# Sparse attention: the token's norm factor moves from the queries into distances, maximum and the exponential's scale

## What is computed

```python
z = u @ w_in
q, kc, vc, ks, vs, kw, vw, gl = split(z)
qg = q.reshape(T, 4, 4, 128) * 128 ** -0.5          # 16 heads, 4 groups
k_cmp, v_cmp = compress(kc), compress(vc)           # 15 blocks
s = qg . k - slope[head] * dist                     # for k_cmp, ks, kw; masked where dist < 0
o = g0 * softmax(s_cmp) @ v_cmp + g1 * softmax(s_slc) @ vs + g2 * softmax(s_win) @ vw
```

## Time and profile before

| what | value |
|---|---|
| median of 3 executions | 3325.81 us |
| profiled execution, its time | 3326.84 us |
| its span | 3325.1 us |
| PE busy | 3297.8 us, 99% |
| PE weight loads busy | 2792.7 us, 84% |
| DVE busy | 1981.9 us, 60% |
| ACT busy | 1570.3 us, 47% |
| TensorE's granted clock | 1.0 in all 40 slices |

### The profile page before, as it was taken

How to read it: one execution, slowest core, us unless ns; L and a number is a source line. 1 busy time by engine, 2 the same in 40 slices (tenths; PEclk the granted TensorE clock), 3 DMA queues, 4 the chain that set the end, 5 groups by cost and what they waited for, 6 DMA issues and landing times.

```text
span 3325.1 us, 40632 instructions
## 1 busy us (share of the span) xinstructions
PE 3297.8 (99%) x16736; PEld 2792.7 (84%) x16736; DVE 1981.9 (60%) x2606; ACT 1570.3 (47%) x2168; POOL 66.3 (2%) x67
## 2 busy tenths in 40 slices
PE   9999999999999999999999999999999999999998
PEld 8888888888889888878888888888888888888887
DVE  5875665565767856674544445574778645444455
ACT  5573444454553544564444444453555534444443
POOL 0000000000001010000000000000000000000000
PEclk9999999999999999999999999999999999999999
DMA  6454445554543434455555555555423555555554
GB/s 258 157 208 184 173 151 190 182 190 171 185 177 129 156 123 152 165 195 186 190 197 195 190 179 201 190 202 187 152 103 131 194 194 190 191 192 187 197 178 157
DMA packets 84057, 592.49 MB, mean 178 GB/s; under 512 B 9313, under 2 KB 10081, under 8 KB 13345
## 3 DMA queue, kind: packets, MB, share of 16 engines
q1 hardware_dynamic: 81584, 576.23, 47.8%
q0 software_dynamic: 2288, 13.67, 1.1%
HBM read 587.76 MB, written 2.10 MB: 177 GB/s over the span
## 4 chain that ended last, share of the span: by engine, by line
PE 93%; DVE 3%; ACT 2%; issue 1%; DMA 0%; POOL 0%; SPq 0%; POOLq 0%; DVEq 0%; ACTq 0%
PE ps L2773 91%; DVE wlo L1538 1%; PE ps L3627 1%; ACT whi L673 1%; ACT sq L691 1%; PE ps L2954 0%; DVE l L2388 0%; DVE xx L1682 0%; ACT l4s L1445 0%; PE ps L3602 0%; DMA raw<-in_ev_in 0%; DVE xres L1843 0%; PE ps L3051 0%; ACT xx L770 0%; DVE l4s L2656 0%
## 5 line engine op out<-in xcount | busy, mean ns | idle before, releaser
L1538 DVE TENSOR_TENSOR wlo<-raw,whi 128x1024 fp32r<-128x1024 f32 x1089 | 1307.4, 1220 | 840.2 <-ACT whi L673 839.1
L2773 PE MATMUL ps<-whi,xx 128*128 128x512 f32 x5184 | 1655.1, 394 | 2.6 <-DVE wlo L1538 1.5
L673 ACT ACTIVATE whi<-raw 128x1024 fp32r<-128x1024 f32 x1089 | 1129.0, 1055 | 902.3 <-PE ps L2773 799.2
L2773 PEld LDWEIGHTS ps<-whi,xx 128*128 128x128 f32 x5184 | 973.6, 188 | 205.8 <-DVE wlo L1538 4.0
L2773 PE MATMUL ps<-wlo,xx 128*128 128x512 f32 x2592 | 1009.5, 389 | 0.0
L2773 PE MATMUL ps<-xx,whi 128*128 128x512 f32 (+3 forms) x2464 | 629.5, 373 | 3.1 <-ACT whi L680 2.0
L2773 PEld LDWEIGHTS ps<-wlo,xx 128*128 128x128 f32 x2592 | 487.5, 188 | 94.8
L2773 PEld LDWEIGHTS ps<-xx,whi 128*128 128x128 f32 (+2 forms) x2464 | 408.5, 187 | 51.9 <-issue 3.6
L2773 PE MATMUL ps<-xx,wlo 128*128 128x256 f32 x2160 | 378.7, 281 | 0.0
L2773 PEld LDWEIGHTS ps<-xx,wlo 128*128 128x128 f32 x2160 | 337.4, 187 | 40.4
L2773 PE MATMUL ps<-whi,fhh 128*128 128x512 f32 x704 | 274.7, 390 | 0.0
(11 more groups left out here) (367 smaller groups left out, 1690.6 us busy)
## 6 DMA issues: line engine op xcount, KB each, us to landing
raw<-in_ffn_gu SPq DMA_DIRECT2D x176, 1024.0 KB, 4.8
raw<-in_ffn_down SPq DMA_DIRECT2D x88, 1024.0 KB, 4.8
raw<-in_ab_in SPq DMA_DIRECT2D x64, 1024.0 KB, 4.8
raw<-in_ev_in SPq DMA_DIRECT2D x62, 1024.0 KB, 4.9
raw<-in_od_in SPq DMA_DIRECT2D x48, 1024.0 KB, 4.8
raw<-in_nsa_in SPq DMA_DIRECT2D x40, 1024.0 KB, 4.8
raw<-in_ev_out SPq DMA_DIRECT2D x16, 1024.0 KB, 4.8
raw<-in_od_out SPq DMA_DIRECT2D x16, 1024.0 KB, 4.7
```

The costliest lines, as they stand in the source:

```text
L673: self.e.activation(m.hi[i % NSPLIT][:, 0:w], m.raw[t % NRAW][:, off:off + w], ACT.Copy).then_inc(*self.up("hi", i))
L1538: self.e.tensor_tensor(m.lo[i % NSPLIT][:, 0:w], m.raw[t % NRAW][:, off:off + w], m.hi[i % NSPLIT][:, 0:w].bitcast(F32), SUB).then_inc(*se ...
L2773: return self.e.matmul(out, l, r, start=start, stop=stop, skip_group_check=True)
```

## The change

The queries stay as `x * gain @ w`, without the factor r of their token and without 128 ** -0.5. The scores are then too large by `1 / (r * SQ)` for each token, with SQ = 128 ** -0.5. So the slopes are divided by `r * SQ` (a column for each head and token tile, made once), the maximum is multiplied by `-r * SQ` in place of -1, and the exponential gets `r * SQ` as its scale. The multiplication L1788 falls away for the queries; the scores wait for the sum in place of the product. Masked distances are 1e27 in place of 1e32, and compressed rows that have no valid key get distance 0.

```diff
+    slopes = np.broadcast_to(-np.asarray(SLOPE2) / SQ, (128, 16))
...
-    big = 1e32
+    big = 1e27
...
-                    e.activation(ap, ap, ACT.Exp, bias=mx[:, i:i + 1], accum_out=den[:, i:i + 1]).then_inc(
-                        *self.up("l4_exp", it, i))
+                    e.activation(ap, ap, ACT.Exp, bias=mx[:, i:i + 1], scale=m.cell(2, "l4_up")[:, it % 2:it % 2 + 1],
+                                 accum_out=den[:, i:i + 1]).then_inc(*self.up("l4_exp", it, i))
...
+        if raw:
+            return
         self.wait_ge("summed", tag, nb, q, 1)
...
         self.finish()
+        self.score_factors()
         self.bg(self.attention4(), R4[0])
...
-                (self.evict_later if i else self.evict_pair)(m.l4_q[:, i * 4 + 2 * q:i * 4 + 2 * q + 2, :], "l4_q", i, q, SQ)
+                (self.evict_later if i else self.evict_pair)(m.l4_q[:, i * 4 + 2 * q:i * 4 + 2 * q + 2, :], "l4_q", i, q,
+                                                             raw=True)
...
+    def score_factors(self):
+
+        m, e = self.m, self.e
+        r, root = m.cell(2, "rs", "x4"), m.cell(2, "l4_root")
+        slope = m.cell(32, "l4_slope").rearrange("p (a h) -> p a h", a=2)
+        self.wait_ge("rstd", "x4")
+        e.reciprocal(root, r).then_inc(*self.up("l4_factor", "root"))
+        e.tensor_scalar(m.cell(2, "l4_up"), r, SQ, None, MUL).then_inc(*self.up("l4_factor", "up"))
+        e.tensor_scalar(m.cell(2, "l4_down"), r, -SQ, None, MUL).then_inc(*self.up("l4_factor", "down"))
+        self.wait_ge("l4_factor", "root")
+        e.tensor_tensor(slope, bc(m.cst[:, C_SLOPE:C_SLOPE + 16].unsqueeze(1), [128, 2, 16]),
+                        bc(root.unsqueeze(2), [128, 2, 16]), MUL).then_inc(*self.up("l4_factor", "slope"))
...
+                slope = m.cell(32, "l4_slope")[:, 16 * qt + h:16 * qt + h + 1]
                 self.wait_ge("l4_scores", it)
                 self.wait_ge("l_dm4")
+                self.wait_ge("l4_factor", "slope")
...
-                e.scalar_tensor_tensor(out=s3, in0=bc(dm[:, mo:mo + nk].unsqueeze(1), [128, 2, nk]), scalar=-SLOPE2[h],
+                e.scalar_tensor_tensor(out=s3, in0=bc(dm[:, mo:mo + nk].unsqueeze(1), [128, 2, nk]), scalar=slope,
...
-                e.scalar_tensor_tensor(out=sc, in0=dm[:, 384 + qt * 16:384 + qt * 16 + 15], scalar=-SLOPE2[h],
+                e.scalar_tensor_tensor(out=sc, in0=dm[:, 384 + qt * 16:384 + qt * 16 + 15], scalar=slope,
...
-                e.tensor_scalar(mx, mx, -1.0, None, MUL).then_inc(*self.up("l4_soft", it, "neg"))
+                e.tensor_scalar(mx, mx, m.cell(2, "l4_down")[:, qt:qt + 1], None, MUL).then_inc(
+                    *self.up("l4_soft", it, "neg"))
...
-                self.wait_ge("scaled", "l4_q", g, 1)
+                self.wait_ge("summed", "l4_q", g, 1, 1)
```

More of the change, by code:

```diff
@@ L30 @@
 C_GAIN = 128
+C_SLOPE = 144
 C_TRI = 256
@@ L65, in constants @@
     t = np.arange(128)[None, :]
-    parts = [np.eye(128), gain, np.zeros((128, 112)), s <= t, np.ones((128, 128))]
+    slopes = np.broadcast_to(-np.asarray(SLOPE2) / SQ, (128, 16))
+    parts = [np.eye(128), gain, slopes, np.zeros((128, 96)), s <= t, np.ones((128, 128))]
     for level in range(7):
@@ L85, in distances @@
             d = base + np.arange(128)[:, None] - (16 * np.arange(15)[None, :] + 31)
-            v = (d >= 0) if keep else np.where(d >= 0, d, big)
+            v = (d >= 0) if keep else np.where(d >= 0, d, np.where((d >= 0).any(axis=1, keepdims=True), big, 0))
             out += [v, np.zeros((128, 1))]
@@ L1760, in pair_block, with evict_later @@
             self.evict_pair(outs[q], tag, nb, q, scale)
-    def evict_later(self, out, tag, nb, q, scale=None):
-        self.due.append((out, tag, nb, q, scale))
+    def evict_later(self, out, tag, nb, q, scale=None, raw=False):
+        self.due.append((out, tag, nb, q, scale, raw))
     def step(self):
@@ L1773, in finish, with evict_pair @@
         self.step()
-    def evict_pair(self, out, tag, nb, q, scale=None):
+    def evict_pair(self, out, tag, nb, q, scale=None, raw=False):
         m, e = self.m, self.e
```

## The result

| | before | after |
|---|---|---|
| median of the runs (22 each), us | 3325.64 | 3330.26 |
| lowest and highest, us | 3324.43 to 3327.30 | 3328.88 to 3331.96 |
| span of the profiled execution, us | 3325.1 | 3327.1 |
| from the gates' table load to the next feed-forward's, us | 288.73 | 293.46 |

The ratio is 1.0014, with a 95% interval of 1.0008 to 1.0020: slower by 4.6 us. The interval leaves out 1, so the loss is clear, though it is smaller than the 0.2% that the prediction took as the least change that can be told. The forecast was 3331.0 us and "same".

A forecast was written before the change was run, and what follows sets the result against it. TensorE, busy 99%, is held at 15 places by a ring over three engines. VectorE's and ScalarE's added columns less the removed products, 16d+14a-1.34 = 5.2 us, on 3325.8 gave 3331.0 us, "same"; range 3326.0 to 3335.4 us.

The forecast's parts named there:

- lateness counts once a step in held places: Attention ring: at 15 places where TensorE waits, each nanosecond added counts; lateness ends where VectorE waits for TensorE's scores.
- The sum by runs: Attention stretch, walked between places where VectorE waits for TensorE's scores: added times together 5.2 us.
- a: ScalarE, each attention step: second column on three exponentials, 0.087 us each, adds 0.26 us a step.
- the second column is free: Rival, ScalarE's exponentials: second column costs nothing, about 1.5 us more in all, 3327.3 us; chance 0.13.
- the one at 0.17: Rival, ScalarE's queue: second column costs 0.17 us per exponential, 8.8 us more in all, 3334.6 us; chance 0.22.
- The third rival, that the columns are hidden: Columns cost nothing but the product's removal counts: -1.0 us, 3324.8 us; chance 0.1.
- d: VectorE, each attention step: three scalars become per-token columns, 0.06 us each, adding 0.18 us a step.
- The product: VectorE, queries: eight L1788 go, 0.72 us each; two credited in the sum, at 2350 to 2381 and at 2438.21.
- TensorE's idle time: Edited stretch: TensorE's idle time was to rise from 3.5 to about 8.7 us, most of it after 2440.
- TensorE's idle time of 3.5 us caps any gain: Edited stretch: relief of VectorE or ScalarE cannot gain more than TensorE's 3.5 us idle, so -0.2% is out of reach.
- The marks of held places: TensorE's loads 0.29 us after L2684's start (8 transposes) or 0.31 to 0.38 after L1423's (7 scores) show holds; more expected.
- Four small instructions and the slopes' wait: Ahead of the projections: four instructions of some 0.17 us hidden by VectorE's 2.09 us idle; the wait costs nothing.

The follow-up runs named there:

- e5: Kernel before with a column of ones as scale in the exponentials of attention steps 4 to 12 only: stretch -0.02 us, median 3325.56 us.
- e6: Kernel before with a column of ones as scale in the exponentials of attention steps 13 to 26 only: stretch +3.13 us, median 3328.80 us.
- e1: Kernel before with a column of ones as scale in all 96 exponentials, nothing else: stretch +3.98 us, median 3329.22 us.
- e2: Kernel before with slopes and -1 read from constant columns in VectorE's three instructions of each step, nothing else: stretch +2.11 us, median 3327.56 us.
- e3: Kernel before without the eight products L1788 on the queries, scores waiting for the sum: stretch -1.08 us, median 3324.30 us.
- e4: Changed kernel with constant scales in the exponentials and a column of -1 for the maxima: stretch +0.61 us against before, median 3326.27 us.
- e9: Kernel before with ScalarE's next weight split issued ahead of its wait for the maxima: stretch -3.94 us, median 3321.87 us.
- e8: Changed kernel with ScalarE's copy that frees the scores' bank issued right behind the exponentials: stretch +4.79 us against before, median 3330.25 us.
- e10: Changed kernel with ScalarE's next weight split issued ahead of its wait for the maxima: stretch -2.30 us against before, median 3323.36 us.

## Why the prediction was right

The forecast of 5.2 us more stands against 4.6 by the medians and 4.73 by the stretch. By its steps:

- **That lateness counts once a step in held places, and ends where VectorE waits for scores: shown.** e5 and e6 tell it directly, -0.02 and +3.13 us for the same edit. That TensorE never idles from 2375 to 2431 held too. But lateness ends there earlier than was said: not only the 1.83 us at 2431.66 takes it back, the waits for scores at 2382, 2388 and 2395 do so already (0.80, 0.42 and 0.77 us before), and after stands at 0.27 behind each.
- **The sum by runs**, predicted and then measured as the shift of TensorE's loads for the scores and transposes in after: to 2381, +0.34 and +0.26; to 2431, 0 and 0; 2431 to 2461, +1.22 and +1.09; to 2480, +1.32 and +1.13; to 2505, +1.32 and +1.24; to 2517, +0.88 and +0.84; behind that, +0.1 and +0.17. The points inside the third run came out as walked: -0.17 at 2442 (-0.10 was said), +0.57 at the scores of 2450 (0.60) and +0.67 at the transposes of 2454 (0.78).
- **a, the exponentials' second column: right in kind, a little small.** 0.28 us a step against 0.26, and 3.98 us (e1) where 14 x 0.26 = 3.6 were in the sum. The Trainium skill's 93 ns for each column ("ScalarE: Activation LUTs", section "What ACT_TABLE_LOAD costs") agrees with the 92 and 93 ns here; the row of a first column, 80 to 83 ns, was the poorer guide. The rival "the second column is free" is out, and so is the one at 0.17: no exponential grew by more than 0.093 us. The third rival, that the columns are hidden, is out by e1 and e2, +3.98 and +2.11 us.
- **d, VectorE's three columns: the term that was mis-sized.** The durations came as said (745, 476, 224, 229 ns). But the sum of durations, 0.18, is not what the chain gets: 0.14 (e2), because the instruction of 15 elements hides half of its 60 ns. Over the stretch the columns cost 2.11 us, where 16 x 0.18 = 2.9 were in the sum.
- **The product: -1.08 alone (e3), but the -1.44 of the sum holds where it counts.** The one at 2438.21 gave its 0.72. The one of the first run gave 0.44 alone; in the changed kernel, where the columns stand beside it, e4 and after show its whole 0.72. So the walk with the measured sizes is 16 x 0.14 + 14 x 0.28 - 1.34 = 4.8 us against 4.73: the steps counted fit, d was 0.6 us too dear in the sum and a 0.3 us too cheap. That these two misses pull against each other is luck.
- **TensorE's idle time: right sign, wrong size.** It was to go from 3.5 to 8.7 us, and went to 7.5 in the same work (235.73 - 228.25). Between the table loads after is 4.73 us longer and idles 8.73 instead of 4.77, 3.96 more; the remaining 0.77 us is in TensorE's busy time.
- **"TensorE's idle time of 3.5 us caps any gain": wrong.** It was argued from busy time. e9 gains 3.94 us between 2354 and 2541, inside that stretch, and only 1.90 of it was TensorE's idle time; so some stalls stand in its busy time (2.04 us here), and the idle time did not bound the gain. The chance of "faster" rested on this step; it was not called upon, because the change lengthens the ring.
- **The marks of held places: they spread little.** Transposes at 0.29 us behind the probabilities are 9 in place of 8 (the new one at 2528), the scores' marks are 9 in place of 7 (the new ones at 2486 and 2536). The marks tell where the ring holds TensorE; e8 shows that they do not tell which resource to relieve.
- **Four small instructions and the slopes' wait: nothing.** The first soft part is not late for them, at 2354 it is 0.72 us early by the product.

What stays open: whether e9's gain is the order or the one piece of lead, and why e10 is 1.64 us behind e9 instead of 0.7. The waits left in it, 1.0 us in 2 for the copy and 0.7 in 1 for the probabilities, are 1.2 us more than e9's 0.5; that leaves 0.4 us for stalls inside busy rows, and no run tells why TensorE's scores still wait for two copies there.

## What to carry to other kernels

When an engine that is 99% busy is fed by a ring over others, cost an edit per step of the ring, and count only the steps between a held place and the next wait for that engine: the same 0.28 us was worth 3.13 us in 14 steps and nothing in nine. In this ring the cheapest gain was not a shorter instruction but the order in a queue: work whose inputs are ready, and that another engine waits for, goes ahead of the wait and not behind it (with the lead of one more piece that comes with it here). A scalar that becomes a per-token column is not free, neither as an operand nor three times a step, and trading eight products for 192 column operands (six a step, 32 steps) was a loss here, where six of the eight products were covered.

## What the runs showed of the hardware

- A column in place of a constant costs VectorE 60 to 61 ns an instruction at 3, 15, 256 and 512 elements alike (169 to 229, 163 to 224, 415 to 476, 684 to 745). In the queue the same growth showed from start to start as 0.06 us (512 elements), 0.03 (15) and 0.07 (3 elements, up to the exponential that waits for it).
- A second column costs a ScalarE exponential 92 to 93 ns at 15, 128 and 256 elements, and in its queue it counts in full: three of them moved the following instruction by 0.28 us. On ScalarE the first column shows 80 ns in before, in another operation (418 to 498 at 256 elements).
- TensorE's busy time is not a bound for gains: 1643 matmuls were busy 283.96 us in one order of ScalarE's queue and 281.92 in another, with weight loads busy for the same 244.3 us.
